# Sixteen-head attention: values one pair ahead, one weight rounding more in front, output projection begun at pair 6; latent attention's value products together

## The reference, cut to what matters

```
# attention with latents (A): a = h @ w_a; q from rms_norm(cq) @ w_uq, k and v from rms_norm(ckv) @ w_ukv
h = rms_norm(x, attn_pre_g[0])
s = (q_nope . k_nope + rope(q_rope) . rope(k_rope)) * scale      # per head, 8 heads
p = softmax(where(chunk mask, s, -inf)); o = p @ v; y = o @ w_o
# sixteen-head attention (B): keys and values from the output of layer 0, queries from layer 1
k, v = rms_norm(x, g_src) @ w_kv;  q = rms_norm(x, attn_pre_g[1]) @ w_q
s = q . k * 64 ** -0.5 + bias[head, clipped distance]            # per head, 16 heads of 64
p = softmax(s); o = p @ v; y = o @ w_o
```

## Time and profile before

| | us |
|---|---|
| median of 3 runs | 1985.21 (1984.54 to 1985.5) |
| the profiled execution, its own time | 1981.76 |
| its span, first to last instruction | 1980.0 |
| TensorE busy | 1938.3 (98%) |
| VectorE busy | 958.4 (48%) |
| GpSimd busy | 732.4 (37%) |
| ScalarE busy | 722.6 (36%) |
| latents | 0 to 50 |
| latent attention, four pairs | 65.9 to about 166 |
| sixteen-head attention, eight pairs | 616.5 to 794 |
| its output projection | 794 to about 835 |

### The profile page before, as it was taken

One profiled execution on the slowest core, in us unless ns is written; L12 is line 12 of the kernel. 1 busy time (PEld: TensorE's weight loads), 2 busy tenths in 40 slices (PEclk: granted clock), 3 DMA queues, 4 the chain that ended last, 5 costly groups with the idle time before them and its releaser, 6 DMA issues.

```text
span 1980.0 us, 22714 instructions
## 1 busy us (share of the span) xinstructions
PE 1938.3 (98%) x9094; PEld 1565.8 (79%) x9094; DVE 958.4 (48%) x1649; ACT 722.6 (36%) x1172; POOL 732.4 (37%) x309
## 2 busy tenths in 40 slices
PE   8999999999998999999999999899999999999998
PEld 7777888888886777888888888788677888888887
DVE  7563564441036445264444005894665765555202
ACT  6554422222244444332222224223654343333221
POOL 2333244444441222524444452342112444444442
PEclk9999999999999999999999999999899999999999
DMA  4412122332231222312233231321111222322222
GB/s 161 167 60 79 55 95 98 99 101 96 96 107 54 86 95 75 117 44 96 99 99 100 97 107 65 127 96 55 42 33 54 96 86 97 100 100 97 96 96 86
DMA packets 52152, 178.60 MB, mean 90 GB/s; under 512 B 5680, under 2 KB 5824, under 8 KB 51792
## 3 DMA queue, kind: packets, MB, share of 16 engines
q1 hardware_dynamic: 45776, 164.09, 25.1%
q10 hardware_dynamic: 6272, 13.07, 1.9%
HBM read 175.00 MB, written 6.33 MB: 92 GB/s over the span
## 4 chain that ended last, share of the span: by engine, by line
PE 87%; DVE 6%; ACT 3%; issue 2%; DMA 1%; POOL 1%; SPq 0%; DVEq 0%; ACTq 0%
PE bank L401 24%; PE bank L403 24%; PE bank L402 24%; PE bank L1384 2%; PE bank L1369 1%; PE bank L1137 1%; PE bank L1131 1%; PE bank L1132 1%; PE bank L1770 1%; PE bank L843 1%; PE bank L1347 1%; DVE tmp L1049 1%; PE bank L1040 1%; POOL wlo L385 1%; DMA raw<-stream 1%
## 5 line engine op out<-in xcount | busy, mean ns | idle before, releaser
L385 POOL TENSOR_TENSOR wlo<-raw,whi 128x1024 fp32r<-128x1024 f32 x285 | 684.6, 2403 | 1203.5 <-ACT whi L380 1203.4
L380 ACT ACTIVATE whi<-raw 128x1024 fp32r<-128x1024 f32 x287 | 304.1, 1060 | 851.6 <-PE bank L403 828.2
L401 PE MATMUL bank<-hh,whi 128*128 128x512 f32 x1384 | 545.1, 394 | 7.6 <-POOL wlo L385 6.3
L402 PE MATMUL bank<-hl,whi 128*128 128x512 f32 x1384 | 540.8, 391 | 0.0
L403 PE MATMUL bank<-hh,wlo 128*128 128x512 f32 x1384 | 540.7, 391 | 0.0
L401 PEld LDWEIGHTS bank<-hh,whi 128*128 128x128 f32 x1384 | 261.6, 189 | 71.4 <-issue 14.5
L403 PEld LDWEIGHTS bank<-hh,wlo 128*128 128x128 f32 x1384 | 261.1, 189 | 55.3
L402 PEld LDWEIGHTS bank<-hl,whi 128*128 128x128 f32 x1384 | 261.5, 189 | 53.2 <-issue 0.2
L514 DVE TENSOR_TENSOR tmp<-bank,rs 128x512 f32<-128x512 f32 x154 | 105.3, 689 | 237.8 <-PE bank L403 223.5
L401 PE MATMUL bank<-fh,whi 128*128 128x512 f32 x496 | 192.9, 389 | 0.0
L402 PE MATMUL bank<-fl,whi 128*128 128x512 f32 x496 | 192.9, 389 | 0.0
(11 more groups left out here) (281 smaller groups left out, 2424.8 us busy)
## 6 DMA issues: line engine op xcount, KB each, us to landing
raw<-stream SPq DMA_DIRECT2D x307, 512.0 KB, 3.4
bias_scratch<-rel_scratch ACTq DMA_DIRECT2D x1, 4096.0 KB, 18.9
biasB<-bias_scratch ACTq DMA_DIRECT2D x16, 256.0 KB, 2.8
w<-w_in ACTq DMA_DIRECT2D x2, 1024.0 KB, 5.9
out<-y ACTq DMA_DIRECT2D x8, 256.0 KB, 2.1
x<-x_in SPq DMA_DIRECT2D x3, 512.0 KB, 8.9
x<-x_in SPq DMA_DIRECT2D x2, 256.0 KB, 5.5
cst<-consts_in SPq DMA_DIRECT2D x1, 448.0 KB, 4.3
```

The source lines that it names most:

```text
L380: e.activation(slot[u][0][:, :], raw[u % 2][:, :], ACT.Copy).then_inc(*w_hi.done(u))
L385: e.tensor_tensor(slot[u][1][:, :], raw[u % 2][:, :], slot[u][0][:, :].bitcast(F32), ALU.subtract)\
L401: e.matmul(o, wh, h, start=first, stop=False)
L402: e.matmul(o, wh, l, start=False, stop=False)
```

## The change

1. **Slots**: the third output tile's unit of the sixteen-head attention (118) gets a slot of its own; `join_act` of that stage rounds one unit more, ahead of the first bias loads, and the output projection's extra roundings are in two places in place of three.
2. **Latents**: the squares of `x` go through four banks in place of two; the spreading of the token factors is ahead of block 6 of `a3`, in place of block 2.
3. **Latent attention**: the value products of both heads follow each other, and the transposes of the next pair's values come behind them; ScalarE writes both heads' high parts ahead of copying these values. The last pair waits for its own value copy explicitly.
4. **Sixteen-head attention**: vB(p+2) in place of vB(p+1) is projected in pair p, behind the transposes of the probabilities; kB(p+1) and qB(p+1) come between scores and transposes. Pair 0 has qB1 between scores and transposes; both sets of values are turned in pair 0, in banks 7 and 6.
5. **Output**: pair 6 makes five blocks of output tile 0, pair 7 two more of it and seven blocks of tile 1; tile 2 covers the last pair's rounding.

```diff
...
     FIRST = {"F0": 26, "B": 92, "F1": 124, "C": 190}
-    OWN_AT = {"F0": (72, 80, 64), "B": (0, 8, 16), "F1": (48, 56, 36), "C": (0, 8, 16)}
+    OWN_AT = {"F0": (72, 80, 64), "B": (0, 8, 16), "F1": (48, 56, 36, 40), "C": (0, 8, 16)}
     slot, before, last_in = [], [], {}
     for u in range(n_units):
-        own = [(n, i) for n in FIRST for i, d in enumerate(((-4, 0), (-3, 1), (3,))) if u - FIRST[n] in d]
+        own = [(n, i) for n in FIRST for i, d in zip(range(len(OWN_AT[n])), ((-4, 0), (-3, 1), (3,), (-6,))) if u - FIRST[n] in d]
         if own:
...
         for n, b in FIRST.items():
-            i = {-4: 1, -3: 3, 3: 5}.get(u - b)
+            i = {-4: 1, -3: 3, 3: 5, -6: 7 if n == "F1" else None}.get(u - b)
             if i is not None and n in ("B", "C"):
...
+    X_THROUGH = (bank[6], bank[7], bank[3], bank[4])
...
         project(e, 2, hh, hl, ("a", 2), between={2: lambda: latent_sums_pe(e, "x", ("x", "sq", KD - 1), tmp[7])})
-        project(e, 3, hh, hl, ("a", 3), between={2: lambda: spread_tokens_pe(e, 4, "x", 48)})
+        project(e, 3, hh, hl, ("a", 3), between={6: lambda: spread_tokens_pe(e, 4, "x", 48)})
         e.wait_ge(*made.at(("x", "inv")))
...
                 round_unit(e)
-            square_tile(e, "x", k, x[:, k, :], bank[6:8])
+            square_tile(e, "x", k, x[:, k, :], X_THROUGH)
         round_unit(e)
...
         for k in range(1, KD):
-            add_square(e, "x", k, bank[6:8])
+            add_square(e, "x", k, X_THROUGH)
             dve_table(e, next(tables))
...
                 e.wait_ge(*low.at(("A", p - 1, 1)))
+                e.wait_ge(*spread.at(("v1", p)))
                 out_blocks_pe(e, u, 0, (0, 1, 2))
...
             mla_times_v_pe(e, p, 0)
+            if not more:
+                out_blocks_pe(e, u, 0, (5,))
+            mla_times_v_pe(e, p, 1)
             if more:
...
                 mla_values_pe(e, p + 1, 1)
-            else:
-                out_blocks_pe(e, u, 0, (5,))
-            mla_times_v_pe(e, p, 1)
         return u
...
             more = p + 1 < NA
-            if p:
-                mla_out_act(e, p - 1, 1)
             mla_exp_act(e, p)
...
             mla_out_act(e, p, 0)
+            mla_out_act(e, p, 1)
             if more:
                 mla_values_act(e, p + 1)
-        mla_out_act(e, NA - 1, 1)
...
-    def out_pe(e, key, u, done):
-        last = ("A", NA - 1, 1) if key == "oA" else ("B", PAIRS_B - 1)
-        us = (u, next_unit(e))
-        out_blocks_pe(e, us[1], 1, (0, 1, 2))
-        e.wait_ge(*low.at(last))
-        for i, k in enumerate((done, 3)):
-            out_blocks_pe(e, us[i], i, range(k, KD)).then_inc(*proj.done((key, i), ("unit", us[i])))
-        for m in range(2, KD):
+    def out_pe(e, key, begun, ahead):
+        n = len(begun)
+        u = next_unit(e)
+        out_blocks_pe(e, u, n, range(ahead))
+        e.wait_ge(*low.at(("A", NA - 1, 1) if key == "oA" else ("B", PAIRS_B - 1)))
+        for m, (um, done) in enumerate(begun + [(u, ahead)]):
+            out_blocks_pe(e, um, m, range(done, KD)).then_inc(*proj.done((key, m), ("unit", um)))
+        for m in range(n + 1, KD):
             u = next_unit(e)
...
             round_unit(e)
-            if m in (1, 2, 3):
+            if m in ((1, 2, 3) if key == "oA" else (1, 6)):
                 round_unit(e)
...
+    VALUES_IN = (7, 6) + (5,) * (PAIRS_B - 2)
+    def values_of(p):
+        return tmp[7] if p == 1 else vtmpB
...
-        e.wait_ge(*evicted.at(("vB", p) if p else ("kB", 1)))
+        e.wait_ge(*evicted.at(("vB", p)))
         for t in range(QT):
-            mm = e.transpose(bank[5 if p else 7][:, t * P:(t + 1) * P], vtmpB[:, t * P:(t + 1) * P], ident)
+            mm = e.transpose(bank[VALUES_IN[p]][:, t * P:(t + 1) * P], values_of(p)[:, t * P:(t + 1) * P], ident)
         mm.then_inc(*turned.done(("vB", p)))
...
         e.wait_ge(*turned.at(("vB", p)))
-        e.activation(vB[p % 2][:, :, :], bank[5 if p else 7][:, :].rearrange("p (k c) -> p k c", c=P), ACT.Copy).then_inc(*spread.done(("vB", p)))
+        e.activation(vB[p % 2][:, :, :], bank[VALUES_IN[p]][:, :].rearrange("p (k c) -> p k c", c=P), ACT.Copy).then_inc(*spread.done(("vB", p)))
...
     def b_first_act(e):
-        join_act(e, "j1", "kvsrc", (bank[2], bank[4]), "pre1", False)
+        join_act(e, "j1", "kvsrc", (bank[2], bank[4]), "pre1")
         load_bias(e, 0, 0)
         load_bias(e, 0, 1)
-        b_values_act(e, 0)
...
         dve_scale(e, 7, rs[0], kB[1][:, :], ("kB", 1))
+        dve_scale(e, 5, rs[0], values_of(1)[:, :], ("vB", 1))
...
             pair_scores_pe(e, ("B", p), qB[p % 2], kB[p % 2])
-            if more:
-                if p == 0:
-                    b_values_pe(e, 0)
-                else:
-                    project(e, 5, hh, hl, ("vB", p + 1))
-                if p:
-                    e.wait_ge(*stats.at(((("B", p), 1), "min", 1)))
-                    project(e, 6, hh, hl, ("kB", p + 1))
+            if p == 0:
+                e.wait_ge(*evicted.at(("vB", 1)))
+                project(e, 5, h2h, h2l, ("qB", 1))
+                b_values_pe(e, 0)
+                e.wait_ge(*stats.at(((("B", 0), 1), "min", 1)))
+                b_values_pe(e, 1)
+                e.wait_ge(*spread.at(("vB", 0)))
+            elif more:
+                e.wait_ge(*evicted.at(("vB", p + 1)))
+                project(e, 5, hh, hl, ("kB", p + 1))
+                e.wait_ge(*stats.at(((("B", p), 1), "min", 1)))
+                project(e, 6, h2h, h2l, ("qB", p + 1))
+                e.wait_ge(*evicted.at(("kB", p + 1)))
                 b_values_pe(e, p + 1)
             else:
-                u = next_unit(e)
                 e.wait_ge(*low.at(("B", p - 1)))
-                out_blocks_pe(e, u, 0, range(6))
+                out_blocks_pe(e, u, 0, (5, 6))
+                e.wait_ge(*stats.at(((("B", p), 1), "min", 1)))
+                u1 = next_unit(e)
+                out_blocks_pe(e, u1, 1, range(4))
             if p:
...
             if more:
-                e.wait_ge(*spread.at(("vB", p + 1)))
-                project(e, 5, h2h, h2l, ("qB", p + 1))
+                e.wait_ge(*(spread.at(("vB", p + 1)) if p else evicted.at(("qB", 1))))
+            if p + 2 < PAIRS_B:
+                project(e, 5, hh, hl, ("vB", p + 2))
+            elif more:
+                u = next_unit(e)
+                out_blocks_pe(e, u, 0, range(5))
             else:
-                out_blocks_pe(e, u, 0, (6,))
+                out_blocks_pe(e, u1, 1, (4, 5, 6))
             pair_times_v_pe(e, ("B", p), lambda k, h: vB[p % 2][:, k, 64 * h:64 * h + 64], PTB)
-        return u
+        return u, u1
...
                 round_unit(e)
+            if p == 0:
+                b_values_act(e, 0)
+            if more:
                 b_values_act(e, p + 1)
...
             b_mins_dve(e, p, 1)
-            if more:
-                e.wait_ge(*proj.at(("vB", p + 1)))
-                if p == 0:
-                    e.wait_ge(*turned.at(("vB", 0)))
-                dve_scale(e, 5, rs[0], vtmpB[:, :], ("vB", p + 1))
+            if p and more:
+                e.wait_ge(*proj.at(("kB", p + 1)))
+                dve_scale(e, 5, rs[0], kB[nb][:, :], ("kB", p + 1))
             dve_normalise(e, (("B", p), 0), probsB[0], 0)
...
             if more:
-                if p:
-                    e.wait_ge(*proj.at(("kB", p + 1)))
-                    dve_scale(e, 6, rs[0], kB[nb][:, :], ("kB", p + 1))
                 e.wait_ge(*proj.at(("qB", p + 1)))
-                dve_scale(e, 5, rs[0], qB[nb][:, :], ("qB", p + 1))
+                dve_scale(e, 6 if p else 5, rs[0], qB[nb][:, :], ("qB", p + 1))
+            if p + 2 < PAIRS_B:
+                e.wait_ge(*proj.at(("vB", p + 2)))
+                e.wait_ge(*turned.at(("vB", p + 1 if p else 0)))
+                dve_scale(e, 5, rs[0], vtmpB[:, :], ("vB", p + 2))
             e.wait_ge(*mixed.at(("B", p)))
...
         u = mla_pe(e)
-        out_pe(e, "oA", u, 6)
+        out_pe(e, "oA", [(u, 6)], 3)
         join_pe(e, "j0", ((2, ("F0", "gate", 0), False), (3, ("F0", "up", 0), False), (0, ("F0", "gate", 1), False),
...
         ffn_pe(e, "F0", False)
-        u = b_pe(e)
-        out_pe(e, "oB", u, 7)
+        u, u1 = b_pe(e)
+        out_pe(e, "oB", [(u, 7), (u1, 7)], 3)
         join_pe(e, "j2", ((2, ("F1", "gate", 0), False), (3, ("F1", "up", 0), False), (0, ("F1", "gate", 1), False),
```

## The result

| | before | after |
|---|---|---|
| median, us | 1984.88 (4 runs, 1983.27 to 1985.5) | 1971.13 (4 runs, 1969.92 to 1971.61) |
| ratio, 95% interval | | 0.9931, 0.9914 to 0.9948 |
| profiled execution, its own time and span | 1981.76, 1980.0 | 1971.61, 1969.8 |

The change makes the kernel 13.8 us faster (10.3 to 17.1 by the interval). The forecast was 1975.3 with a range from 1972.3: the direction was right, the gain was under-estimated by 3.9 us, and the result lies 1.2 us under the range. Yet the two profiled executions differ by 10.2 us, close to the 9.9 forecast. The two profiles and the two medians do not tell the same, and that turned out to be a part of the matter.

A forecast was written before the change was run, and what follows sets the result against it. TensorE, busy 98% of the span, was taken to bound the kernel. Gains 2.4 + 2.2 + 5.0 + 0 + 0.3 = 9.9 us, taken from the median 1985.2, gave 1975.3 us, range 1972.3 to 1979.2.

The forecast's parts named there:

- Latents: In the latents, the pauses at a2's low part and at the spread go: 2.4 us, ends 0 and 2.7.
- Latent attention: In three latent-attention pairs, a value product covers the 0.71 us wait ahead of transposes: 2.2 us, lower end 0.
- Pair 0, the new order: Sixteen heads, first pair after the change: needs 18.8 us, takes 22.3, with new waits of 1.8 and 1.7.
- normalising held by GpSimd: In pair 0, GpSimd's low part of unit 99 blocks VectorE's normalising of head 1: second new TensorE wait, 1.7 us.
- Pair 0, the old order: Sixteen heads, first pair before the change: needs 13.3 us, takes 21.82, so 8.5 lost, partly at the half clock.
- the term of pair 0: First pair of the sixteen heads: 3.5 us lost in place of 8.5, gain 5.0, ends 6.8 and 3.3.
- the clock falls in pair 0 as well: Rival: after the change the granted clock falls in the sixteen heads' pair 0; gain 8.2 us, 1977.0, chance 0.20.
- missed meeting: Rival: in pair 0, GpSimd's low part misses the normalising of head 1; gain 11.7 us, 1973.5, chance 0.12.
- Middle pairs: Sixteen heads, pairs between first and last: bound by TensorE, each rounding waits for the same place as before; 0 us.
- pair 7: Last sixteen-head pair and output: new 0.9 us wait, shorter waits elsewhere; sum +0.3 us, ends -0.6 and +0.6.
- pairs 1 to 6 at 23.9: Sign that the forecast is right: in the sixteen heads these pairs take 23.9 us each.
- the upper latents term: Upper end of the gain in the latents, 2.7 us; joined with the missed meeting in the range as 12.9.

The follow-up runs named there:

- sixteen heads alone: Kernel before with only the sixteen-head part: slot, added rounding, values a pair ahead, output blocks; 1976.87 us, ratio 0.9956.
- the repeat: Kernel before, unchanged, measured and profiled again; 1985.7 us, ratio 1.0003, profiled execution 1987.14 us.
- latents alone: Kernel before with only the squares through four banks and the later spreading; 1983.12 us, ratio 0.9988.
- latent attention alone: Kernel before with only the value products of both heads together in the latent attention; 1980.43 us, ratio 0.9979.
- only the spreading: Kernel before with only the spreading moved ahead of block 6 of a3, squares still through two banks; one execution, first scores 1.4 us earlier.
- four with the edits: Changed kernel with bias loads ahead of rounding, value copies ahead of rounding, both, or both plus output blocks four and three; 1971.76, 1968.14, 1969.5, 1968.3 us.
- the repeat's interval: Changed kernel, unchanged, measured again against the kernel before; 1970.6 us, ratio 0.9927, 14.7 us faster (12.1 to 16.9).

## Why the prediction was wrong

- **Latents.** Mechanism right, both pauses went; 2.0 us, not 2.4. Two small pauses came (0.28, 0.23), the second where the prediction had seen a low part due within 0.1 us.
- **Latent attention.** Mechanism right: the product covers the wait, nothing returns at the scores. The term was mis-sized: 2.2 forecast, 3.3 measured, in the change and alone. The brackets of the earlier trace rows were taken for the price; the pause here also cost the run-out of the matmul ahead, the slow first matmuls behind it and one more change of kind (0.16, 0.12 and 0.09 us).
- **Pair 0, the new order.** The chain was the forecast one, in its order: bias behind the rounding, copy behind the next rounding, normalising held by GpSimd. Forecast 22.3, measured 21.08; the two pauses are 1.15 and 0.61 us and not 1.8 and 1.7. Timeline of ScalarE after:

```profile
612.31 1.06 ACT L381 ACTIVATE whi<-raw 128x1024 fp32r<-128x1024 f32 x1 [4.27 <-PE bank L404]
612.34 0.85 ACTq L1399 DMA_DIRECT2D biasB<-bias_scratch  x2
613.39 1.28 ACT L451 ACT_TABLE_LOAD   x1
...
620.71 1.04 ACT L381 ACTIVATE whi<-raw 128x1024 fp32r<-128x1024 f32 x1
621.65 1.06 ACT L1416 ACTIVATE vB<-bank 128x512 f32<-128x512 f32 x2
```

  The bias loads are issued at 612.34, with the rounding and not after it, 0.2 us after the first scores where the prediction looked for 1.2. The changed kernel's second profile and that of the sixteen heads alone show the same 0.03 us. On VectorE:

```profile
615.04 0.83 DVE L1421 TENSOR_SCALAR biasB<-biasB 64x64 f32<-64x64 f32 x1 [1.50 <-DMA biasB<-bias_scratch]
...
621.04 3.43 DVE L466 TENSOR_SCALAR probsB<-probsB,stat 128x128 f32<-128x128 f32 x4
```

  and on GpSimd:

```profile
613.45 2.37 POOL L386 TENSOR_TENSOR wlo<-raw,whi 128x1024 fp32r<-128x1024 f32 x1 [4.48 <-ACT whi L381]
621.82 2.37 POOL L386 TENSOR_TENSOR wlo<-raw,whi 128x1024 fp32r<-128x1024 f32 x1 [6.01 <-ACT whi L381]
```

  The bias lands 2.9 us after the scores' start (4.0 forecast). The mask then takes 0.83 us where the like took 0.18, next to the low part of unit 98 on GpSimd: a second meeting, which was not foreseen. The first came as forecast, 3.43 us. Most of the earlier bias is lost again on the way: the low part of unit 99 starts 9.7 us after the scores, against 10.0 in the prediction. The rest of the 1.2 us lies behind it. The prediction let the normalising end 0.9 us after that low part (629.8 against 628.9), while its own rows have 0.28 (626.18 + 3.41 against 626.96 + 2.35) and the trace after 0.28; and it gave the last transposes 1.15 us, where they took 0.8.
- **Pair 0, the old order.** "Before, pair 0 needs ... 13.3 and takes 21.82 ... 8.5 us lost, partly at the half clock": that was one execution, with 3.4 us at the half clock that lay ahead of a wait and cost nothing, and its gain was then taken off a median. In five profiles with the old pair 0 (the one before, the repeat, latents alone, latent attention alone, only the spreading) it took 21.82, 24.53, 21.82, 23.43 and 23.23 us, 23.0 in the mean; in seven with the new order (two of the changed kernel, sixteen heads alone, four with the edits) no stretch at the half clock lies in it.
- **The step that failed** is the term of pair 0, 5.0 us. It measured 6.2 between the two first profiles, by the shorter new order, and 7.4 in the mean (23.0 + 5.5 - 21.1), by the longer old one: two errors of 1.2 us each, both on the same side. The latent attention's 1.1 us is the third. With 2.0, 3.3 and 0.2 the sum is 12.9, against 9.9 forecast and 13.8 and 14.7 measured; both intervals take it in. Without the old order's share it would be 11.7, just below the repeat's interval (12.1 to 16.9).
- **What stays open** is 1 to 2 us. Beside the table above, the two unchanged rows together took 1614.5 to 1619.1 us in the five profiles with the old pair 0 (1616.2 in the mean) and 1613.3 to 1618.1 in the seven with the new one (1615.0). That is a scatter as large as the open rest, with stretches at the half clock at differing places, so neither a further gain nor its absence is shown.
- The rival "the clock falls in pair 0 as well" was priced for the new order and never for the old one, whose own loss was read as fixed. It did not happen in any profile of the new order. That 11.7 us by the marks is the figure of the rival "missed meeting" is luck: the meeting took place.
- **Middle pairs, pair 7.** 0 for the middle pairs: right, pairs 1 to 5 at 23.86 each. The sign "pairs 1 to 6 at 23.9" was wrong for pair 6 by the prediction's own plan, which puts five blocks there for a unit: 21.82. Pair 7: a new pause of 0.69 (0.9 forecast), the pause at the third tile gone, sum +0.2 (+0.3 forecast).
- **The range.** Its upper gain, 12.9, does not follow from its words: the missed meeting with the upper latents term is 11.7 + 0.3 = 12.0, which would have put the end at 1973.2.
- The median stood 3.45 us above the profiled execution and the prediction named this, but did not ask why. By the table of executions the clock goes along: 0.991 in the profiled one, 0.989 in most.

The Trainium skill (TensorE: Matmul & The Clock Gate, section Part 1: The HAM clock gate) says that where the clock changes depends on the run, since it is not tied to the kernel's start. The runs here agree that it depends on the run: the same code of pair 0 took between 21.82 and 24.53 us, with 3.4 to 13.65 us at the half clock. They do not show the reason.

## What to carry to other kernels

A stretch with pauses of 1.1 to 2.7 us on TensorE had here a price that differed by 2.7 us from execution to execution, since the clock fell in it and, in some executions, stayed down into the work behind its last wait; ask how often the profiled execution is the cheap one before its loss is put into a sum, and compare its mean granted clock with that of the timed runs. Read a pause from start to start, not from its bracket: here 0.71 us in the bracket were 1.1 us in time. When work was moved ahead of loads on the same engine, the loads stood behind its wait, not behind its duration (issued 0.03 us after its start). And compare the stages that a change does not touch: here they differed by up to 5.8 us between profiles, which is more than any of its small terms.

## What was not expected of the hardware

- The clock stood at the half level for 13.65 us, and its last 4 us lay across dense work: in the repeat of the kernel before, qB1 ran in it from 632 to 636 with TensorE busy 4.00 of 4.00 us (window above).
- Transfers on ScalarE's queue were issued while the activation ahead of them ran: 612.34 against 612.31 to 613.37.
- A 64x64 scalar operation of 0.18 us on VectorE took 0.83 us while GpSimd formed a low part.
- A filler `matmul` of 128x128 in float32 cost two records and 0.23 us (18 of them 4.1 us), as much as one of 512 columns in the rounded format (0.227).
